# A fused two-block kernel on one core: key norms inverted with tokens on partitions, two gate projections inside the first RWKV tile, the rest of the RG-LRU spread over tiles 1 to 6

## The chip, the cores and the metric

The kernel is written for one core of a Trainium2 chip, and nothing else runs. The metric is the device time of one execution in microseconds (us), lower is better. The engines are named as in the profile: PE is TensorE (matrix products), PEld its weight loads, DVE is VectorE, ACT is ScalarE, POOL is GpSimd, SP is SyncE, which issues most of the transfers. Each works through its own list of instructions in order; semaphores tie them together.

## The reference, cut to what matters

Two model blocks run one after the other on 1024 tokens of width 1024, in float32. The change lies in the first. It projects the tokens, mixes them in three ways side by side (windowed attention, RG-LRU, RWKV-7), gates each with the silu of a projection, projects out and normalises. The two ways that the change touches:

```python
# RG-LRU (256 channels)
xc = causal_conv(xb, width 4) + conv_b
r, i = sigmoid(xc @ wa + ba), sigmoid(xc @ wx + bx)      # blocks of 64
log_a = -8 * r * softplus(-lam);  a = exp(log_a)
u = sqrt(-expm1(2 * log_a)) * (i * xc)
h[t] = a[t] * h[t-1] + u[t]                               # scan over tokens
# RWKV-7 (4 heads of 64)
kk = k * k_k
kk = kk * rsqrt(sum(kk ** 2 over a head) + 1e-12)
k = k * (1 + (a - 1) * k_a)
state = state * w + (state @ -kk) b^T + v k^T;  y = state @ r     # b = kk * a
bonus = sum(r * k * r_k over a head) * v
out = concat(y_a * silu(g_a), h * silu(g_b), (norm(y) + bonus) * silu(g_c)) @ w_out
```

The second block (pooling mixer, latent attention, two layers of routed experts) takes the rest of the time and is not touched.

## The kernel before

Data of the first block lie with channels on partitions and the 1024 tokens along the free axis, as two tiles (`j` = 0, 1) of 128 channels each. Three stages matter, and every engine has a function for each.

**Attention with projections beside it** (`pe_swa` and others) ends near 338 us. `proj` lists all projections, each a group of eight float32 products of 128x512 accumulated in one of two PSUM banks (ring `pj`). The last six, `left[0]` to `left[5]`, are gates. `act_project` takes the sigmoid of one, and `dve_project` multiplies it (line 379), which frees the bank.

**Preparation** (`pe_prep`, `act_prep`, `dve_prep`) works on whole 128x1024 tensors. PE does, in this order: `left[0]`; sums of squares of `kk` over a head (four products with `pair_ones`, ring `pr_`, six banks); eight products for the decay and `a` (`DECAY`); `left[1]`, four products of the RG-LRU's two gates for `j` = 0 (`LRU_MM`), `left[2]`, four for `j` = 1, `left[3]`, `left[4]`, two for the bonus (`rk`), `left[5]`, two more. DVE does the convolution (`dve_conv`, lines 777 and 780), the reciprocal of the norms (798), the running sum of the log decay (803) and the products with decays (820 to 825), a 128x1024 instruction each. ACT takes roots (747), sigmoids (752, 761), exponentials (764 to 768), and the RG-LRU's tanh and exp (771, 772). `after_prep` is what all three wait for before the next stage.

**RWKV tiles** (`pe_rwkv`, `act_rwkv`, `dve_rwkv`): eight tiles of 128 tokens. `rounds()` gives the order: tile `i` does steps 0 to 9 (its front: products of 64x64 that invert a triangular matrix) in rounds 10i to 10i+9, and in the same rounds tile `i`-1 does steps 10 to 19 (its back: the state recurrence and the norm). So tile 0's rounds hold a front alone. Between two rounds' products PE waits for a copy on ACT (1205) or a combination on DVE (1271). Step 0 begins with four masks on DVE (1259, 1265), behind the previous tile's step 19, a reciprocal (1356) that waits for a root on ACT (1240). `dve_lru` and `act_lru` put what is left of the RG-LRU between these, all with `i` = 0: products 848, 852, 854 and 859 in steps 0 to 8, the scans (863) in steps 9 and 11, the last products (867) in steps 13 and 16. Steps 10 and above fall in tile 1's rounds. When the RG-LRU is done (`lru_v`), SP loads the output weights, eight transfers of 512 KB (`sp_rwkv`). Tile 7 waits for them from step 10 on and does part of the output projection between its steps.

Of the kernel before, what the change touches and what calls it, by code (L numbers as in the profile page):

```python
# [170 lines left out]
def build(nc, io):  # L171
    ctx = ExitStack()
    with ctx:
# [164 lines left out]
        def pe_project(e, n):  # L338
            group, c0, width, half, kind, _ = proj[n]
            if n == first_of[group]:  # L340
                e.wait_ge(*m_w[group])
# [296 lines left out]
        def sp_first(e):  # L638
# [13 lines left out]
            for name, before in (("rk", None), ("vwa", "ga"), ("lru", "rk"), ("gc", "vwa")):  # L652
                if before:
# [37 lines left out]
        order = [(("kk", j, hf), "S") for j in range(2) for hf in range(2)] + [(("wa",) + x, "S") for x in DECAY]  # L691
        order += [(("lru",) + x, "S") for x in LRU_MM] + [(("rk", j, hf), "V") for j in range(2) for hf in range(2)]
        pr_ = Banks(banks[:6], *sw.rest(), order)
        reset_in, masks_in, lru_zero = signal("reset"), signal("rwkv_masks"), signal("lru_zero")
# [4 lines left out]
        assert len(left) == 6

        def pe_prep(e):
            pe_project(e, left[0])
            wait_all(e, after_swa)
            for j in range(2):
# [23 lines left out]
            for j in range(2):  # L728
                e.wait_ge(*rk_in.at(j + 1))
                for hf in range(2):  # L730
                    key = ("rk", j, hf)
                    wait_all(e, pr_.free(key))
                    mm(e, pr_.bank[key], pair_ones, tmp[j][:, half_cols(hf)], True, True).then_inc(*pr_.fill(key))
                if j == 0:
                    pe_project(e, left[5])

        def act_prep(e):
            wait_all(e, after_swa)
            for j in range(2):
                e.wait_ge(*kk_raw.at(j + 1))  # L740
                e.activation(Lc[:, j, :], kk[:, j, :], ACT.Square).then_inc(*kk_sq.up())
            act_project(e, left[0])
            for j in range(2):
                for hf in range(2):
                    key = ("kk", j, hf)
                    e.wait_ge(*pr_.full(key))
                    e.activation(tmp[j][:, half_cols(hf)], pr_.bank[key], ACT.Sqrt, bias=eps_kk).then_inc(*pr_.drain(key, "S"))
            for j, what, hf in DECAY:
# [3 lines left out]
                e.activation(dst[:, j, half_cols(hf)], pr_.bank[key], ACT.Sigmoid, bias=col(bias, j)).then_inc(*pr_.drain(key, "S"))  # L752
            for j in range(2):
# [2276 lines left out]
```

## Time and profile before

| | |
|---|---|
| runs | 2324.21, 2327.46, 2329.42 us; median 2327.46 |
| profiled execution | 2327.86 us, its span 2326.1 us |
| PE busy | 2114.3 us, 91% of the span |
| DVE, ACT, POOL busy | 826.3, 559.5, 198.5 us |
| preparation | from about 346 to 415 us |
| RWKV tiles | from 415 to about 605 us |

The span is the time from the first to the last instruction in the profiled execution. A float32 product shows as two PE records. The granted clock is a share of TensorE's full speed: 1.00 is 2.4 GHz, 0.50 is 1.2 GHz.

### The profile page before, as it was taken

The page shows a single profiled execution, that of the slowest core. Times are in us where ns is not written, and L with a number is a line of the kernel's source. Part 1 is how long each engine was busy: PE and PEld are TensorE (multiplying, and loading weights), DVE is VectorE, ACT ScalarE, POOL GpSimd, SP SyncE. Part 2 cuts the span into 40 slices and gives each one's busy share as a digit, 9 for nine tenths or more (in the row PEclk, how much of TensorE's full clock was granted, in tenths as well). Part 3 has the DMA queues.
Part 4 walks back from the last instruction along what each step waited for, and adds up shares of the span by engine and source line. Part 5 has one row for each costly group of instructions (what it writes and reads, how often), then busy time and mean ns, then how long its engine had stood idle before and what let it go on. Part 6 is the DMA issues. An engine that isn't in the chain of part 4 may idle for free. (4 is left out here: it accounts for less than half of the span.)

```text
span 2326.1 us, 27337 instructions
## 1 busy us (share of the span) xinstructions
PE 2114.3 (91%) x10876; PEld 1217.8 (52%) x10876; DVE 826.3 (36%) x1833; ACT 559.5 (24%) x1349; POOL 198.5 (9%) x297
## 2 busy tenths in 40 slices
PE   8999999789989669999987999999999849999991
PEld 4545554687438344444434657767764324444440
DVE  1115549664344332111125533443431141111115
ACT  1013235332113201112213433333321101111112
POOL 0000002011432010000002000000000000000003
PEclk9999999899989779999998999999999869999996
DMA  3501000100211359999963000000100067999966
GB/s 127 217 23 37 19 2 3 74 4 3 70 60 44 124 218 369 384 408 367 365 241 125 21 0 1 1 1 1 73 13 36 36 253 299 367 367 366 370 271 245
DMA packets 46199, 349.30 MB, mean 150 GB/s; under 512 B 6256, under 2 KB 6576, under 8 KB 36208
## 3 DMA queue, kind: packets, MB, share of 16 engines
q1 hardware_dynamic: 32176, 296.97, 32.5%
q0 software_dynamic: 13888, 50.47, 6.2%
q8 instruction: 92, 1.51, 0.3%
q14 instruction: 43, 0.35, 0.0%
HBM read 292.82 MB, written 54.59 MB: 149 GB/s over the span
## 5 line engine op out<-in xcount | busy, mean ns | idle before, releaser
L202 PE MATMUL psum<-arena 128*128 128x512 f32 (+7 forms) x9328 | 1956.8, 384 | 113.9 <-DVE arena L1923 25.9
L202 PEld LDWEIGHTS psum<-arena 128*128 128x128 f32 (+3 forms) x9328 | 1046.0, 169 | 955.1 <-issue 831.5
L2054 DVE TENSOR_TENSOR arena<-psum,arena 128x256 f32<-128x256 f32 x64 | 27.2, 425 | 539.9 <-ACT arena L2098 539.9
L2134 POOL DMA_INDIRECT arena<-xn_rows,arena x64 | 60.2, 941 | 818.7 <-PE psum L2021 587.4
L2098 ACT ACTIVATE arena<-psum 128x256 f32<-128x256 f32 x64 | 24.6, 384 | 400.9 <-PE psum L202 400.9
L1475 ACT ACTIVATE arena<-arena 128x1024 f32<-128x1024 f32 x43 | 45.4, 1056 | 250.9 <-DVE arena L2789 101.6
L2702 ACT ACTIVATE arena<-psum,arena 128x1024 f32<-128x1024 f32 (+8 forms) x72 | 50.2, 699 | 188.6 <-DVE arena L2738 188.6
L2091 ACT ACTIVATE arena<-psum 128x512 f32<-128x512 f32 x64 | 38.2, 597 | 185.5 <-PE psum L202 185.5
L2021 PE MATMUL psum<-arena 128*128 128x128 f32 x512 | 68.2, 277 | 9.8 <-DMA arena<-xn_rows,arena 9.8
L1205 ACT ACTIVATE arena<-psum 128x256 f32<-128x256 f32 (+3 forms) x128 | 45.6, 369 | 106.8 <-PE psum L202 96.7
L2121 DVE COPY arena<-psum 128x512 f32<-128x512 f32 x64 | 44.3, 692 | 61.5 <-PE psum L202 61.5
L2021 PEld LDWEIGHTS psum<-arena 128*128 128x128 f32 x512 | 59.3, 144 | 11.2 <-DMA arena<-xn_rows,arena 10.1
L2079 ACT ACTIVATE arena<-psum 128x512 f32<-128x512 f32 x64 | 38.2, 598 | 93.2 <-PE psum L2021 93.2
L2731 DVE TENSOR_TENSOR psum<-psum,arena 128x128 f32<-128x128 f32 (+2 forms) x72 | 20.3, 282 | 103.5 <-PE psum L202 103.2
L2733 DVE TENSOR_REDUCE arena<-psum 128x1 f32<-128x1024 f32 (+8 forms) x72 | 50.8, 706 | 2.5
L2242 DVE SCALAR_TENSOR_TENSOR arena<-arena 128x1024 f32<-128x1024 f32 (+1 forms) x34 | 43.5, 1280 | 21.4 <-DMA arena<-expert_rows,arena 19.7
L2754 DVE COPY arena<-psum 128x512 f32<-128x512 f32 (+3 forms) x48 | 22.8, 490 | 76.0 <-PE psum L2657 75.9
L2248 POOL DMA_INDIRECT arena<-expert_rows,arena x34 | 34.4, 1012 | 178.9 <-issue 126.3
L2657 PE MATMUL psum<-arena 128*128 128x128 f32 x352 | 48.9, 273 | 0.0
L2114 DVE COPY arena<-psum 128x512 f32<-128x512 f32 x64 | 43.5, 680 | 11.6 <-PE psum L2021 11.6
L365 ACT ACTIVATE arena<-psum 128x512 f32<-128x512 f32 (+1 forms) x26 | 15.5, 597 | 128.5 <-PE psum L202 128.5
L379 DVE TENSOR_TENSOR arena<-psum,arena 128x512 f32<-128x512 f32 x16 | 10.9, 689 | 87.5 <-ACT arena L360 87.4
(286 smaller groups left out, 1288.9 us busy)
## 6 DMA issues: line engine op xcount, KB each, us to landing
arena<-in_w_exp SPq DMA_DIRECT2D x64, 3072.0 KB, 11.7
expert_rows<-arena SPq DMA_DIRECT2D x80, 512.0 KB, 4.1
arena<-in_x SPq DMA_DIRECT2D x16, 512.0 KB, 4.2
xn_rows<-arena SPq DMA_DIRECT2D x16, 512.0 KB, 2.6
arena<-in_w_out SPq DMA_DIRECT2D x8, 512.0 KB, 7.9
arena<-in_w_o SPq DMA_DIRECT2D x1, 4096.0 KB, 12.0
out<-arena SPq DMA_DIRECT2D x8, 512.0 KB, 5.8
arena<-in_rows SPq DMA_DIRECT2D x6, 512.0 KB, 6.3
```

The lines of the kernel that those rows point to most:

```text
L202: return e.matmul(out, lhsT, rhs, start=start, stop=stop, skip_group_check=True)
L1205: e.activation(dst, src, ACT.Copy, bias=0.0).then_inc(*ring.drain((i, name), "S"))
L1475: return e.activation(junk, h[:, s, :], ACT.Square, accum_out=sq_sum[:, s:s + 1])
L2021: m = e.transpose(four(ring.bank[key])[:, k, :], xe[:, P * (4 * hf + k):P * (4 * hf + k + 1)], ident)
L2079: e.activation(y.xt[b % 2][:, 4:8, :], four(y.ex.bank[key]), ACT.Copy, bias=0.0).then_inc(*y.ex.drain(key, "S"))
L2114: e.tensor_copy(y.xt[b % 2][:, 0:4, :], four(y.ex.bank[key])).then_inc(*y.ex.drain(key, "V"))
L2121: e.tensor_copy(y.y[b % 3][:, half_cols(0)], y.ex.bank[key]).then_inc(*y.ex.drain(key, "V"))
L2134: e.indirect_dma_start(out=xe, out_offset=None, in_=xn_dram[:, :], in_offset=bass.IndirectOffsetOnAxis(idx.bitcast(I32)[:, block:block + 1 ...
L2242: e.scalar_tensor_tensor(out=h[0:n, s, :], in0=c[j][0:n, :], scalar=gates[0:n, s, j:j + 1], in1=h[0:n, s, :], op0=ALU.mult, op1=ALU.add).t ...
L2657: m = e.transpose(four(sd.bank[key])[:, j, :], pb[:, kp:kp + P], ident)
L2702: e.activation(pb[0:n, p0:p1], part_bank(key).bank[key][0:n, 0:p1 - p0], ACT.Exp, bias=mx[0:n, 0:1], scale=SCALE, accum_out=rsu[0:n, u:u + ...
L2733: e.tensor_reduce(mx[0:n, u:u + 1], bk[0:n, 0:p1 - p0], AX.X, ALU.max).then_inc(*V.up())
```

## The change

Norms of the keys: the squares (ACT now takes them from `k` itself, with `k_k` as its scale) become the stationary operand of sixteen narrow products against two columns of `pair_ones`, so 32 sums per token lie in one bank with tokens on partitions (`kn`). Root and reciprocal then run on 128x32. ACT widens the result to 128x1024 twice (`kk_b`, in the memory of `Em`), and sixteen products with the identity turn it back into four PSUM banks (`kk`), which DVE multiplies into `kk`. The first tap of the convolution moves from DVE to ACT. ACT's exponentials now stand ahead of the RG-LRU's sigmoids, and tanh and exp leave the stage. The bonus products stand before `left[2]`. `left[4]` and `left[5]` move into tile 0: two products at the head of each of steps 1 to 8, sigmoid and multiplication at step 9. The rest of the RG-LRU moves to tiles 1 to 6 by two tables. The names of memory areas change with it, and the waits of tile 1 for `lru_u` go.

```diff
+def pe_project(e, n, part=range(KD)):
-    wait_all(e, pj.free(n))
+    if part[0] == 0:
+        wait_all(e, pj.free(n))
-    for k in range(KD):
+    for k in part:
         i = mm(e, out, w_view[group][:, k, c0:c0 + width], xT[:, k, half_cols(half)], k == 0, k == KD - 1)
+    if part[-1] == KD - 1:
+        i.then_inc(*pj.fill(n))
...
+order = [("kn", "S")] + [(("wa",) + x, "S") for x in DECAY] + [(("kk", j, hf), "V") for j in range(2) for hf in range(2)]
+for j in range(2):
+    order += [(("lru",) + x, "S") for x in LRU_MM if x[1] == j]
+    if j == 0:
+        order += [(("rk", jj, hf), "V") for jj in range(2) for hf in range(2)]
...
+LATE = left[4:]
+LATE_AT = {step: (LATE[(step - 1) // 4], range(2 * ((step - 1) % 4), 2 * ((step - 1) % 4) + 2)) for step in range(1, 9)}
...
-        e.wait_ge(*kk_sq.at(j + 1))
-        for hf in range(2):
-            key = ("kk", j, hf)
-            wait_all(e, pr_.free(key))
-            mm(e, pr_.bank[key], pair_ones, Lc[:, j, half_cols(hf)], True, True).then_inc(*pr_.fill(key))
+    e.wait_ge(*kk_sq.at(2))
+    wait_all(e, pr_.free("kn"))
+    for t in range(NT):
+        for j in range(2):
+            m = mm(e, pr_.bank["kn"][:, 4 * t + 2 * j:4 * t + 2 * j + 2], Lc[:, j, P * t:P * (t + 1)], pair_ones[:, 0:P:HD], True, True)
+    m.then_inc(*pr_.fill("kn"))
...
+    pe_project(e, left[1])
+    e.wait_ge(*kk_wide.at(2))
     for j in range(2):
-        pe_project(e, left[1 + j])
+        for hf in range(2):
+            key = ("kk", j, hf)
+            wait_all(e, pr_.free(key))
+            for u in range(4):
+                c = 4 * (4 * hf + u) + 2 * j
+                m = mm(e, four(pr_.bank[key])[:, u, :], kk_b[:, c:c + 2, :].rearrange("p a b -> p (a b)"), ident, True, True)
+            m.then_inc(*pr_.fill(key))
...
+    for j in range(2):
+        if j:
+            pe_project(e, left[2])
...
+        if j == 0:
+            for jj in range(2):
+                e.wait_ge(*rk_in.at(jj + 1))
+                for hf in range(2):
+                    key = ("rk", jj, hf)
+                    wait_all(e, pr_.free(key))
+                    mm(e, pr_.bank[key], pair_ones, tmp[jj][:, half_cols(hf)], True, True).then_inc(*pr_.fill(key))
     pe_project(e, left[3])
-    pe_project(e, left[4])
...
-        e.activation(Lc[:, j, :], kk[:, j, :], ACT.Square).then_inc(*kk_sq.up())
+        e.activation(Lc[:, j, :], R[2 + j], ACT.Square, scale=col("k_k", j)).then_inc(*kk_sq.up())
+    e.wait_ge(*pj.full(last_of["vwa"]))
+    for j in range(2):
+        e.wait_ge(*pj.empty(last_half["xb", j]))
+        e.activation(xc[:, j, :], xb[:, j, 0:T], ACT.Identity, bias=col("conv_b", j), scale=col("conv_w", 4 * j)).then_inc(*conv_in.up())
...
+    e.wait_ge(*pr_.full("kn"))
+    e.activation(kk_dev, pr_.bank["kn"][:, 0:4 * NT], ACT.Sqrt, bias=eps_kk).then_inc(*pr_.drain("kn", "S"))
...
+    e.wait_ge(*kk_in.at(1))
+    for c in (0, 2 * NT):
+        e.activation(kk_b[:, c:c + 2 * NT, :], bc_last(kk_r[:, c:c + 2 * NT], HD), ACT.Copy, bias=0.0).then_inc(*kk_wide.up())
+    for j in range(2):
+        e.wait_ge(*scanned.at(j + 1))
+        e.activation(Ep[:, j, :], Lc[:, j, :], ACT.Exp, scale=-EXP_HALF).then_inc(*exped.up())
+        e.wait_ge(*pr_.full(("kk", 1, 1)))
+        e.activation(Em[:, j, :], Lc[:, j, :], ACT.Exp, scale=EXP_HALF).then_inc(*exped.up())
+    for j in range(2):
+        e.wait_ge(*to_exp.at(j + 1))
+        e.activation(sgm[:, j, :], sgm[:, j, :], ACT.Exp, scale=-EXP_HALF).then_inc(*exped.up())
...
-        e.wait_ge(*pr_.empty(("lru", "x", 1, 1)))
-        e.activation(q_[:, j, :], ra[:, j, :], ACT.Tanh, scale=ncl[:, j:j + 1]).then_inc(*S.up())
-        e.activation(ra[:, j, :], ra[:, j, :], ACT.Exp, scale=cl[:, j:j + 1]).then_inc(*lru_a.up())
-    for n in left[3:]:
-        act_project(e, n)
+    act_project(e, left[3])
...
-    e.tensor_scalar(xc[:, j, :], xb[:, j, 0:T], col("conv_w", 4 * j), col("conv_b", j), ALU.mult, ALU.add).then_inc(*V.up())
+    e.wait_ge(*conv_in.at(j + 1))
...
-        dve_conv(e, j)
-        if j == 0:
-            dve_project(e, left[0])
+        e.tensor_scalar(kk[:, j, :], R[2 + j], col("k_k", j), None, ALU.mult).then_inc(*V.up())
...
+    e.wait_ge(*pr_.empty("kn"))
+    e.reciprocal(kk_r, kk_dev).then_inc(*kk_in.up())
...
-        e.reciprocal(tmp[j], tmp[j]).then_inc(*V.up())
-        e.wait_ge(*V.last())
-        e.tensor_tensor(kk[:, j, :], kk[:, j, :], tmp[j], ALU.mult).then_inc(*V.up())
...
-        e.tensor_tensor(av[:, j, :], av[:, j, :], kk[:, j, :], ALU.mult).then_inc(*V.up())
...
+    for j in range(2):
+        for hf in range(2):
+            key = ("kk", j, hf)
+            kc = kk[:, j, half_cols(hf)]
+            e.wait_ge(*pr_.full(key))
+            e.tensor_tensor(kc, pr_.bank[key], kc, ALU.mult).then_inc(*pr_.drain(key, "V"))
...
+    for j in range(2):
+        e.tensor_tensor(av[:, j, :], av[:, j, :], kk[:, j, :], ALU.mult).then_inc(*V.up())
+    dve_bonus(e, 0)
...
+LRU_ACT = {(1, 2): ("tanh", 0), (1, 4): ("decay", 0), (1, 6): ("tanh", 1), (1, 8): ("decay", 1), (3, 6): ("sqrt", 0), (4, 2): ("sqrt", 1)}
+LRU_DVE = {(1, 4): ("gate", 0), (1, 9): ("gate", 1), (2, 4): ("square", 0), (2, 9): ("rest", 0), (3, 4): ("square", 1), (3, 9): ("rest", 1),
+           (4, 4): ("input", 0), (4, 9): ("scan", 0), (5, 2): ("input", 1), (5, 4): ("scan", 1), (5, 9): ("out", 0), (6, 2): ("out", 1)}
...
+after_prep = pr_.totals + [pj.empty(left[3]), (prep_v.sem, 2), (exped.sem, 6), (rk_in.sem, 2), m_lru]
...
+        if i == 0 and s in LATE_AT:
+            pe_project(e, *LATE_AT[s])
+        if (i, s) == (0, 10):
+            wait_all(e, pj.totals)
...
+        act_lru(e, i, s)
+        if (i, s) == (0, 9):
+            for n in LATE:
+                act_project(e, n)
...
+        dve_lru(e, i, s)
+        if (i, s) == (0, 9):
+            for n in LATE:
+                dve_project(e, n)
+            e.memset(STt[:, 0], 0.0).then_inc(*states.up())
```

In the diff, `dve_bonus(e, j)` holds the two multiplications of line 832, unchanged. `gate`, `square`, `rest`, `input`, `scan` and `out` are the operations of lines 848, 852, 854, 859, 863 and 867.

How the instructions stand on PE from the end of attention to tile 1. Before (80 products of 128x512 are the preparation; L1078 are tile transposes):

```order
L202 MATMUL psum<-arena 128x512 x80
L202 MATMUL psum<-arena 64x64 x16
L1078 MATMUL psum<-arena 128x128 x8
L202 MATMUL psum<-arena 64x64 x152
L1078 MATMUL psum<-arena 128x128 x8
L202 MATMUL psum<-arena 64x64 x184
```

In the changed kernel:

```order
L202 MATMUL psum<-arena 128x512 x16
L202 MATMUL psum<-arena 128x2 x16
L202 MATMUL psum<-arena 128x512 x16
L202 MATMUL psum<-arena 128x128 x16
L202 MATMUL psum<-arena 128x512 x28
L202 MATMUL psum<-arena 64x64 x16
L1120 MATMUL psum<-arena 128x128 x8
L202 MATMUL psum<-arena 128x512 x2
L202 MATMUL psum<-arena 64x64 x16
L202 MATMUL psum<-arena 128x512 x2
L202 MATMUL psum<-arena 64x64 x24
```

The preparation has 20 wide products fewer and 32 small ones more, and 16 of the wide ones stand in pairs within tile 0 (the first two pairs are shown).

DVE in tile 0, after the masks of step 0. Before:

```order
L848 TENSOR_TENSOR arena<-arena 128x1024
L1289 TENSOR_TENSOR arena<-arena 128x256
L1276 COPY arena<-psum 128x256
L848 TENSOR_TENSOR arena<-arena 128x1024
L1265 TENSOR_TENSOR arena<-psum,arena 128x3x128 x2
L852 TENSOR_TENSOR arena<-arena 128x1024
L854 SCALAR_TENSOR_TENSOR arena<-arena 128x1024
L1276 COPY arena<-psum 128x256
```

In the changed kernel the 128x1024 instructions are gone there (same operations, other line numbers):

```order
L1328 TENSOR_TENSOR arena<-arena 128x256
L1317 COPY arena<-psum 128x256
L1306 TENSOR_TENSOR arena<-psum,arena 128x3x128 x2
L1317 COPY arena<-psum 128x256
L1312 TENSOR_TENSOR arena<-arena,psum 128x256 x3
```

DVE in tile 2 of the changed kernel, rounds 4 to 9, where two of them now stand (889 and 892; before, there was none in tile 2):

```order
L1312 TENSOR_TENSOR arena<-arena,psum 128x256
L889 TENSOR_TENSOR arena<-arena 128x1024
L1358 SCALAR_TENSOR_TENSOR arena<-psum,arena 64x128 x2
L1312 TENSOR_TENSOR arena<-arena,psum 128x256
L1369 SCALAR_TENSOR_TENSOR arena<-psum,arena 128x64 x2
L1377 TENSOR_SCALAR arena<-arena 128x64 x2
L1384 TENSOR_TENSOR arena<-psum,arena 128x2x64 x2
L1389 SCALAR_TENSOR_TENSOR arena<-psum,arena 128x2x128
L1312 TENSOR_TENSOR arena<-arena,psum 128x512
L892 SCALAR_TENSOR_TENSOR arena<-arena 128x1024
L1395 RECIPROCAL arena<-arena 128x256
```

One stands between a front combination and the recurrence's copy, the other ahead of the norm's reciprocal.

## Rows read from the trace of the kernel before

**Rows 1.** Timeline of PE: start us, us, instruction, idle before and its releaser

```profile
402.26 11.93 PE L202 MATMUL psum<-arena 128*128 128x512 f32 x20 [3.68 <-DVE arena L379]
415.12 0.69 PE L202 MATMUL psum<-arena 64*64 64x64 f32 x32 [0.93 <-DVE arena L832]
...
424.04 1.61 PE L202 MATMUL psum<-arena 64*64 64x64 f32 x48 [2.55 <-issue]
```

**Rows 2.** Windows: PE, PEld, DVE, ACT, POOL busy, granted clock, DMA share, GB/s

```profile
360.50:363.00 2.50, 2.50 (x4) 1.08 (x4) 2.50 (x1) 2.14 (x4) 1.89 (x9) 0.54 0.03 7
402.00:404.00 2.00, 1.74 (x2) 0.84 (x3) 2.00 (x4) 0.00 (x0) 0.00 (x0) 0.50 0.00 0
465.00:469.00 4.00, 1.93 (x39) 1.93 (x40) 0.93 (x3) 0.08 (x1) 0.00 (x0) 0.69 0.02 6
```

**Rows 3.** Windows from the first mask of one tile to the next, tiles 0 to 6

```profile
415.90:437.30 21.40, 13.95 (x319) 12.56 (x319) 16.66 (x22) 7.26 (x13) 0.00 (x0) 0.81 0.01 2
437.30:456.80 19.50, 17.41 (x483) 15.79 (x481) 15.70 (x35) 7.30 (x20) 0.00 (x0) 0.95 0.18 55
456.80:477.90 21.10, 16.76 (x468) 15.46 (x464) 11.65 (x33) 6.45 (x19) 2.31 (x4) 0.92 0.39 154
477.90:495.30 17.40, 15.57 (x470) 14.33 (x468) 11.62 (x32) 6.53 (x19) 2.31 (x4) 1.00 0.02 4
495.30:512.90 17.60, 15.57 (x472) 14.50 (x468) 11.58 (x32) 6.59 (x19) 2.31 (x4) 1.00 0.02 4
512.90:530.00 17.10, 15.59 (x472) 14.50 (x468) 11.51 (x32) 6.58 (x19) 2.30 (x4) 1.00 0.01 4
530.00:547.10 17.10, 15.67 (x472) 14.57 (x468) 11.51 (x32) 6.58 (x19) 2.31 (x4) 1.00 0.01 3
```

**Rows 4.** Groups by form on PE, 100 to 110 us: busy us, mean ns, idle

```profile
L202 PE MATMUL psum<-arena 128*128 128x512 f32 x15 | 6.6, 592 | 0.0
L202 PE MATMUL psum<-arena 128*128 128x128 f32 x37 | 4.3, 275 | 0.0
```

**Rows 5.** Timeline of ACT in the preparation

```profile
369.43 0.60 ACT L360 ACTIVATE arena<-psum 128x512 f32<-128x512 f32 x1 [6.79 <-PE psum L202]
370.29 0.69 ACT L761 ACTIVATE arena<-psum,arena 128x512 f32<-128x512 f32 x1 [0.26 <-PE psum L202]
...
383.87 1.28 ACT L764 ACT_TABLE_LOAD   x1
...
387.07 1.04 ACT L764 ACTIVATE arena<-arena 128x1024 f32<-128x1024 f32 x1
388.02 1.04 ACT L765 ACTIVATE arena<-arena 128x1024 f32<-128x1024 f32 x1
```

**Rows 6.** Timeline of DVE in the preparation

```profile
358.19 6.55 DVE L798 RECIPROCAL arena<-arena 128x1024 f32<-128x1024 f32 x1
...
392.43 1.23 DVE L820 TENSOR_TENSOR arena<-arena 128x1024 f32<-128x1024 f32 x1
```

**Rows 7.** Timeline of DVE in tile 3: rounds 34 and 35, then round 39

```profile
485.96 0.42 DVE L1271 TENSOR_TENSOR arena<-arena,psum 128x256 f32<-128x256 f32 x1
486.41 0.50 DVE L1319 SCALAR_TENSOR_TENSOR arena<-psum,arena 64x128 f32<-64x128 f32 x2
487.40 0.42 DVE L1271 TENSOR_TENSOR arena<-arena,psum 128x256 f32<-128x256 f32 x1 [0.49 <-PE psum L202]
...
493.18 1.75 DVE L1356 RECIPROCAL arena<-arena 128x256 f32<-128x256 f32 x1 [0.35 <-ACT arena L1240]
```

**Rows 8.** Timelines of DVE and PE: a scan in tile 1, the wait at tile 3's start

```profile
440.49 2.28 DVE L863 TENSOR_TENSOR_SCAN arena<-arena 128x1024 f32<-128x1024 f32 x1
...
479.38 2.90 PE L202 MATMUL psum<-arena 64*64 64x64 f32 x123 [1.15 <-DVE arena L1265]
```

**Rows 9.** Timeline of PE in tile 2, and the issues of the output weights

```profile
467.07 3.13 PE L202 MATMUL psum<-arena 64*64 64x64 f32 x58 [2.33 <-issue]
...
arena<-in_w_out SPq DMA_DIRECT2D x8, 512.0 KB, 7.9
```

More of the change, by code:

```diff
@@ L666, in build @@
         reset = take(T)
-        end_prep = top[0]
+        kk_dev, kk_r = take(4 * NT), take(4 * NT)
+        kk_b = Em.rearrange("p a b -> p (a b)").rearrange("p (a b) -> p a b", b=HD)
+        assert top[0] <= base_sums
         yb = Lc
@@ L816, in dve_prep @@
                                        op1=ALU.mult).then_inc(*rk_in.up())
+            for j in range(2):
[4 more added lines that the diff above has]
+                    e.tensor_tensor(kc, pr_.bank[key], kc, ALU.mult).then_inc(*pr_.drain(key, "V"))
+            dve_project(e, left[1])
+            e.wait_ge(*pr_.empty(("kk", 1, 1)))
+            for j in range(2):
+                e.tensor_tensor(av[:, j, :], av[:, j, :], kk[:, j, :], ALU.mult).then_inc(*V.up())
+            dve_bonus(e, 0)
             e.wait_ge(*rk_in.last())
+            e.wait_ge(*V.last())
             for j in range(2):
@@ L825, in dve_prep @@
                 e.tensor_tensor(kk[:, j, :], kk[:, j, :], sgm[:, j, :], ALU.mult).then_inc(*prep_v.up())
-            for n in left[3:5]:
-                dve_project(e, n)
-            for j in range(2):
-                for hf in range(2):
-                    key = ("rk", j, hf)
-                    e.wait_ge(*pr_.full(key))
-                    e.tensor_tensor(bonus[:, j, half_cols(hf)], pr_.bank[key], R[4 + j][:, half_cols(hf)],
-                                    ALU.mult).then_inc(*pr_.drain(key, "V"))
-                if j == 0:
-                    dve_project(e, left[5])
@@ L837, in act_lru, with dve_bonus @@
-        def act_lru(e, step):
-            if step in (5, 6):
-                j = step - 5
+            dve_bonus(e, 1)
+            dve_project(e, left[2])
+            dve_project(e, left[3])
+        def dve_bonus(e, j):
+            for hf in range(2):
+                key = ("rk", j, hf)
+                e.wait_ge(*pr_.full(key))
+                e.tensor_tensor(bonus[:, j, half_cols(hf)], pr_.bank[key], R[4 + j][:, half_cols(hf)], ALU.mult).then_inc(*pr_.drain(key, "V"))
+        LRU_ACT = {(1, 2): ("tanh", 0), (1, 4): ("decay", 0), (1, 6): ("tanh", 1), (1, 8): ("decay", 1), (3, 6): ("sqrt", 0), (4, 2): ("sqrt", 1)}
@@ new lines, in build, with act_lru @@
+        LRU_DVE = {(1, 4): ("gate", 0), (1, 9): ("gate", 1), (2, 4): ("square", 0), (2, 9): ("rest", 0), (3, 4): ("square", 1), (3, 9): ("rest", 1),
+                   (4, 4): ("input", 0), (4, 9): ("scan", 0), (5, 2): ("input", 1), (5, 4): ("scan", 1), (5, 9): ("out", 0), (6, 2): ("out", 1)}
+        def act_lru(e, i, s):
+            what, j = LRU_ACT.get((i, s), (None, None))
+            if what == "tanh":
+                e.wait_ge(*pr_.empty(("lru", "x", 1, 1)))
+                e.activation(q_[:, j, :], ra[:, j, :], ACT.Tanh, scale=ncl[:, j:j + 1]).then_inc(*S.up())
+            elif what == "decay":
+                e.activation(ra[:, j, :], ra[:, j, :], ACT.Exp, scale=cl[:, j:j + 1]).then_inc(*lru_a.up())
+            elif what == "sqrt":
@@ L841, in act_lru, with dve_lru @@
                 e.wait_ge(*lru_q.at(j + 1))
                 e.activation(q_[:, j, :], q_[:, j, :], ACT.Sqrt).then_inc(*lru_sq.up())
-        def dve_lru(e, step):
-            if step in (0, 1):
-                j = step
+        def dve_lru(e, i, s):
+            what, j = LRU_DVE.get((i, s), (None, None))
+            if what == "gate":
                 e.wait_ge(*pr_.empty(("lru", "x", 1, 1)))
                 e.tensor_tensor(ib[:, j, :], ib[:, j, :], xc[:, j, :], ALU.mult).then_inc(*V.up())
-            elif step in (2, 3):
-                j = step - 2
+            elif what == "square":
@@ L855, in dve_lru @@
                                        op1=ALU.mult).then_inc(*lru_q.up())
-            elif step in (7, 8):
-                j = step - 7
+            elif what == "input":
                 e.wait_ge(*lru_sq.at(j + 1))
-                e.tensor_tensor(ib[:, j, :], ib[:, j, :], q_[:, j, :], ALU.mult).then_inc(*lru_u.up())
-            elif step in (9, 11):
-                j = (step - 9) // 2
-                e.wait_ge(*lru_u.last())
+                e.tensor_tensor(ib[:, j, :], ib[:, j, :], q_[:, j, :], ALU.mult).then_inc(*V.up())
+            elif what == "scan":
+                e.wait_ge(*V.last())
                 e.tensor_tensor_scan(xc[:, j, :], ra[:, j, :], ib[:, j, :], 0.0, ALU.mult, ALU.add).then_inc(*V.up())
-            elif step in (13, 16):
-                j = (step - 13) // 3
+            elif what == "out":
                 e.wait_ge(*V.last())
@@ L1280, in dve_rwkv @@
                         e.wait_ge(*bk_.full((i - 2, "var")))
-                    if i == 1:
-                        e.wait_ge(*lru_u.last())
                     for par in range(2):
```

75 lines of the change are left out of this document (20 added, 55 removed).

## The prediction

> **What bounds the kernel now.** The first view is the whole page: PE is busy for nine tenths of the span, so a change pays only where it takes work, waiting or half-speed time from PE. The change moves work inside one stretch, 346 to 605 us, so the second view is the timeline of PE there. It shows the preparation as nearly unbroken work up to 398.6 us. Then PE waits 3.68 us for DVE, works off ten products in 11.93 us, waits 0.93 us and starts tile 0 at 415.12 [rows 1]. Ten wide products should take ten times two records of 6.6/15 = 0.44 us, that is 8.8 us [rows 4]; the granted clock is 0.50 behind the wait [rows 2], so about 3.1 us are lost to the half clock (1.2 GHz).
>
> The third view is the table of windows by tile [rows 3]. Tiles 3 to 6, which hold no RG-LRU, take 17.1 to 17.6 us, 17.3 in the mean, of which PE is busy 15.6. Tile 0, with a front alone, takes 21.4 with PE busy 13.95 at a mean clock of 0.81. Its waits are for DVE, which works through the RG-LRU's 128x1024 products there: 2.55 us before the product at 424.04 [rows 1]. Tile 1, with both scans, takes 19.5. Tile 2 takes 21.1 without any of the RG-LRU; there PE stands 2.33 us on "issue" while the output weights land, and the clock falls behind it to 0.69 [rows 2, 9]. I take that excess of about 3.7 us as a late instruction fetch behind the burst.
>
> **The preparation.** Work on PE: sixteen wide products of `left[4]` and `left[5]` leave, and four of the norms. A product is 0.88 us, so -14.1 and -3.5. Added are sixteen 128x128 products with the identity at two records of 4.3/37 = 0.116 us, +3.7 [rows 4]. The sixteen narrow ones have two columns, which no row shows. They cannot cost more than the 128-column ones, 3.7 us; from below the 64x64 products run at 3.13 us for 58 records, 0.054 each, or 1.7 us for 32 [rows 9]. Each still has a full weight load, so I take 3.0, near the upper end. The Trainium skill, "TensorE: Matmul & The Clock Gate", section "LDWEIGHTS (loading the stationary operand)", counts the columns of the stationary operand over 1.2 in ns, 107 ns for 128; by it 32 loads would be 3.4 us and the total 0.4 us more. Sum of the work: -14.1 - 3.5 + 3.7 + 3.0 = -10.9.
>
> Waits of PE: before, 3.68 + 0.93 = 4.6. After, DVE no longer sets them: two reciprocals of 6.55 us [rows 6] shrink to one of 128x32, and the 128x1024 products of 1.23 us stay at about their number. But ACT now stands in the way. The exponential into `Em` overwrites `kk_b`, so it must wait for the last identity product. `left[1]`'s sigmoid began at 369.43 [rows 5]; that product ends half a microsecond sooner, the identity products 3.7 later, at 372.6. Then ACT runs five instructions at the 0.95 spacing of the exponentials, a table load of 1.28, the sigmoid of `left[1]` at 0.60 and the first of the RG-LRU at 0.69 [rows 5]: 372.6 + 4.8 + 1.3 + 0.6 + 0.7 = 380.0. The third bonus product needs the bank that this last one frees. PE gets there after four and two wide products, 372.6 + 5.3 = 377.9, and waits 2.1 us, with the hop some 2.3. The last wait, for sigmoid and multiplication of `left[3]`, was 0.93 behind a shorter chain and becomes about 1.7. So 4.0 us of waits, -0.6.
>
> Clock: before 3.1 us lost behind a wait of 3.68. After a wait of 2.33 tile 2 lost 3.7 - 2.3 = 1.4. For 2.3 us I take 1.6, so -1.5. In both kernels there is a dip at 360.5 behind the 32-row products [rows 2]; I leave it equal. Preparation: -10.9 - 0.6 - 1.5 = **-13.0**; from -10.5 (full loss of clock) to -16 (none, narrow products cheap).
>
> **Tile 0.** Its work at full clock is 13.95 x 0.81 = 11.3 us [rows 3]. The late products add 14.1, and stand where PE waited for ACT and DVE, each pair longer (1.8 us) than a combination's return trip of 1.2 (the wait and the 0.42 copies in [rows 7, 8]). Only step 9 has none, 1.1 us of waiting. 11.3 + 14.1 + 1.1 = 26.5 against 21.4: **+5.1**. The clock stays at 1.00, since PE is dense.
>
> **The RG-LRU in tiles 1 to 6.** Ten products of 1.23 us and two scans of 2.28 [rows 6, 8] go between a steady tile's instructions. An inserted one costs its length less the idle time that DVE has at that place. At step 9 DVE has 0.35 us idle before the reciprocal [rows 7], and what follows, the masks, is what PE waits 1.15 us for already [rows 8]. So a product costs 0.8 (spacing 1.15 less 0.35) and a scan 1.85. At step 4 there is no idle ahead of the recurrence's copy at 486.41, and 0.49 after it [rows 7]: 0.65 for a product, 1.7 for the scan. At step 2 I take 0.35, by the same reading. Tile 1 also gets a table load for the root at step 18, behind an exponential: 0.7 more at its end, and 0.7 at its start, where DVE works off `left[4]` and `left[5]` ahead of the masks. ACT's other instructions fall into its idle time. Against [rows 3], from a base of 17.3:
>
> tile 1: 17.3 + 0.7 + 0.65 + 1.5 = 20.15, +0.65
> tile 2: 17.3 + 0.65 + 0.8 = 18.75, -2.35 (the weights' burst leaves it)
> tile 3: the same 18.75, +1.35
> tile 4: 17.3 + 0.65 + 1.85 = 19.8, +2.2
> tile 5: 17.3 + 0.35 + 1.7 + 0.8 = 20.15, +3.05
> tile 6: 17.3 + 0.35 + 3.7 (the burst comes here) = 21.35, +4.25
>
> Together **+9.15**. The RG-LRU's share is 10.75 us of 16.9 us of instructions. From below: tile 1 before holds a scan and two products, 4.7 us, and exceeds 17.3 by 2.2, of which 1.0 is the clock (0.95 of 19.5), so a quarter shows, 4.3 us in all; from above, all but the idle ones, 14. I keep 10.75, since steps 4 and 9 are tighter places than those. The weights are asked for in round 62, and needed in round 80, 31 us later by the tiles' pace, so they cost no wait. What follows 605 us is chained to the last tile, and shifts.
>
> **Sum.** -13.0 + 5.1 + 9.15 = +1.25 us. On the profiled execution's 2327.86 us that is 2329.1; the median of the runs is 0.4 us lower, so I forecast 2328.7: no change that shows. A measurement of this kernel can tell about 0.2%, 4.7 us, from none.
>
> **Rivals.**
> *The clock falls at the long seams.* At the ends of tiles 1 and 4 PE would wait 1.15 + 1.5 = 2.65 and 1.15 + 1.85 = 3.0 us for the masks. Waits of 3.68 and 2.33 us were followed by half speed [rows 1, 2, 9]. Each such fall costs 1.4 to 3.1. With 3.1 at both the time is 2334.9, slower by over 0.2%; it decides once the two falls together pass 3.5 us. For it: the rows. Against: the 1.15 us waits in tiles 3 to 6 leave the clock at 1.00, and these tiles are otherwise dense. 0.34, which also holds costlier insertions.
> *The RG-LRU hides well.* If all twelve cost as little as tile 1 shows, 4.3 us, the time is 2328.7 - 6.45 = 2322.3, faster by 0.2%. For it: tile 1, whose last product at step 16 sits before an idle DVE. Against: the chain at steps 4 and 9. With a preparation at the short end (-16) it is 2319. 0.25 in all.
> *No burst in tile 6.* If the fetch is not late there, 3.7 us go: 2325.0, no change that shows. 0.1, within the forecast's chance.
> *The late projections aren't hidden.* If tile 0 kept its waits, it would be 21.4 + 14.1 less the regained clock of 2.6, 32.9 us, 6.4 more, 2335.1. Against it speaks that each step's waits are on ACT and DVE alone. 0.04, in the slower share.
>
> **Chances and range.** Forecast, within 0.2%: 0.41, its own range 2323 to 2332. Slower 0.34, faster 0.25. Low end 2319 (the hidden RG-LRU and the short preparation), high end 2337 (both falls, and insertions dearer by 2).
>
> **What would show it.** Right: PE's first tile product 13 us earlier than 415.12, at about 402; a wait of 2 us in the bonus products, on ACT; tile 0 at 26 to 27 us with the clock at 1.00; tiles 3 to 5 between 18.5 and 20.5; a wait of 1.9 to 2.0 us for the masks at the ends of tiles 2 and 3; an "issue" gap with the weights' burst in tile 6 and none in tile 2. Wrong: clock below 1.00 in tiles 4 and 5, or tiles 2 to 5 at 17.5.

## The result, and the profile after

The change makes the kernel slower: 2343.15 us (median of 4 runs, 2339.6 to 2345.18) against 2327.76 us of the kernel before in the same session, ratio 1.0067, 95% interval 1.0055 to 1.0079. The forecast was 2328.7, with 2319 to 2337 as its range. The profiled execution is the slowest of the four, 2345.18 us; its span is 2343.5.

I measure the changed stretch from one DVE instruction that both kernels have at the preparation's entry to the first reciprocal behind tile 7 (608.24 us before, 621.44 after). First the entry, in the timeline of DVE before, then after:

```profile
346.64 0.16 DVE L786 TENSOR_SCALAR arena<-arena 128x2 f32<-128x2 f32 x1
```

```profile
346.88 0.16 DVE L812 TENSOR_SCALAR arena<-arena 128x2 f32<-128x2 f32 x1
```

So the stretch is 261.60 us long before and 274.56 after, +12.96. It adds up from four pieces, each from trace marks: preparation to the first mask -10.04, tile 0 +6.46, tiles 1 to 6 +16.28, tile 7 and its close +0.26.

Timeline of PE after, in the preparation and at the tiles' seams (start, us, instruction, wait ahead and its releaser), to be read beside [rows 1, 8, 9]:

```profile
345.44 35.04 PE L202 MATMUL psum<-arena 128*128 128x512 f32 x124
382.84 20.82 PE L202 MATMUL psum<-arena 128*128 128x512 f32 x44 [2.36 <-ACT arena L798]
405.33 0.69 PE L202 MATMUL psum<-arena 64*64 64x64 f32 x32 [1.67 <-issue]
...
455.86 8.66 PE L202 MATMUL psum<-arena 64*64 64x64 f32 x264 [2.08 <-DVE arena L1306]
...
476.00 7.43 PE L202 MATMUL psum<-arena 64*64 64x64 f32 x264 [1.84 <-DVE arena L1306]
...
494.93 8.76 PE L202 MATMUL psum<-arena 64*64 64x64 f32 x264 [1.85 <-DVE arena L1306]
...
516.77 5.64 PE L202 MATMUL psum<-arena 64*64 64x64 f32 x168 [2.89 <-DVE arena L1306]
...
528.89 6.79 PE L202 MATMUL psum<-arena 64*64 64x64 f32 x128 [2.10 <-DVE arena L1358]
...
552.05 4.33 PE L202 MATMUL psum<-arena 64*64 64x64 f32 x100 [1.57 <-issue]
...
559.35 0.58 PE L202 MATMUL psum<-arena 64*64 64x64 f32 x24 [1.92 <-issue]
```

The waits stand where they were forecast, and all but one in the size forecast: the one at tile 2's start is 2.08 us (2.65 forecast). The wait of 2.10 us in the middle of tile 5 was in the sum as 1.7 us of the scan, and was not named as a wait. What is new is in the last columns of the windows (granted clock, DMA share, GB/s):

```profile
354.00:358.00 4.00, 4.00 (x24) 2.88 (x25) 3.93 (x4) 2.29 (x4) 0.00 (x0) 0.77 0.01 4
358.00:366.00 8.00, 8.00 (x16) 3.35 (x13) 4.86 (x4) 5.99 (x10) 2.87 (x5) 0.50 0.02 4
384.00:386.00 2.00, 2.00 (x4) 0.93 (x3) 2.00 (x3) 0.43 (x1) 0.00 (x0) 0.50 0.00 0
456.00:458.00 2.00, 2.00 (x48) 2.00 (x50) 0.74 (x3) 0.39 (x1) 1.03 (x2) 0.50 0.03 8
518.00:520.00 2.00, 2.00 (x57) 2.00 (x58) 0.42 (x1) 0.75 (x3) 0.00 (x0) 0.50 0.00 0
530.00:534.00 4.00, 4.00 (x70) 3.75 (x67) 1.25 (x6) 1.31 (x4) 0.00 (x0) 0.57 0.00 0
```

The clock is at its lower level of 1.2 GHz behind the narrow products (from 356 to 366 us, with PE busy throughout), behind the wait of 2.36 us, and in tiles 2, 4 and 5. Windows by tile, answering to [rows 3], tiles 0 to 6:

```profile
406.13:433.97 27.84, 26.15 (x352) 15.35 (x351) 7.02 (x16) 5.64 (x13) 0.00 (x0) 1.00 0.01 2
433.97:454.35 20.38, 16.82 (x480) 15.15 (x480) 13.86 (x34) 13.23 (x25) 0.00 (x0) 1.00 0.01 4
454.35:474.49 20.14, 16.90 (x464) 15.71 (x464) 13.79 (x35) 6.58 (x18) 2.31 (x4) 0.92 0.01 3
474.49:493.42 18.93, 15.68 (x464) 14.49 (x464) 13.70 (x35) 7.53 (x19) 2.31 (x4) 1.00 0.01 3
493.42:515.25 21.83, 17.16 (x464) 16.00 (x464) 14.89 (x34) 7.53 (x19) 2.30 (x4) 0.92 0.01 3
515.25:539.06 23.81, 18.46 (x464) 17.35 (x464) 15.87 (x36) 6.58 (x18) 2.31 (x4) 0.86 0.01 3
539.06:560.04 20.98, 14.49 (x442) 13.41 (x443) 12.70 (x33) 5.50 (x16) 3.11 (x6) 1.00 0.54 203
```

### The profile page after: what moved, and what is told of

Same layout as the page of the kernel before. It is cut to its first block and busy times, and to the rows that moved or that the text cites. A ratio compares the mean times of both kernels' runs of the same rounds, so it can differ in the third digit from the quotient of the medians.

```text
span 2343.5 us, 27446 instructions
## 1 busy us (share of the span) xinstructions
PE 2126.0 (91%) x10932; PEld 1229.1 (52%) x10932; DVE 812.7 (35%) x1832; ACT 562.3 (24%) x1351; POOL 203.1 (9%) x297
## 5 line engine op out<-in xcount | busy, mean ns | idle before, releaser
L202 PE MATMUL psum<-arena 64*64 64x64 f32 (+9 forms) x9384 | 1969.6, 386 | 116.9 <-DVE arena L1966 25.9
L202 PEld LDWEIGHTS psum<-arena 128*128 128x128 f32 (+3 forms) x9384 | 1058.2, 172 | 958.6 <-issue 845.9
## 6 DMA issues: line engine op xcount, KB each, us to landing
arena<-in_w_exp SPq DMA_DIRECT2D x64, 3072.0 KB, 12.3
```

Source lines behind the costliest of these rows:

```text
L202: return e.matmul(out, lhsT, rhs, start=start, stop=stop, skip_group_check=True)
```

## The experiments

Twelve kernels in three sessions; the kernel before took 2329.52, 2330.09 and 2327.6 us in them (29 runs each). "Stretch" is the length defined above; it and the lengths of tiles come from one profiled execution of each kernel, the times and ratios from all its runs.

### 65 columns in place of 2

```diff
-m = mm(e, pr_.bank["kn"][:, o:o + 2], Lc[...], pair_ones[:, 0:P:HD], True, True)      # o = 4 * t + 2 * j
+m = mm(e, pr_.bank["kn"][:, o:o + 65], Lc[...], pair_ones[:, HD - 1:P], True, True)
```

> The changed kernel, but the sixteen narrow products run against 65 columns instead of 2 (the first two are the same, the other 63 land in columns that are overwritten or not read; the two-column ones took 0.11 us a record, the 128-column ones 0.116, so the time on the engine is the same). Theory N (the two-column products let TensorE fall to its half clock): the half-clock stretch from 356 to 366 us shrinks towards that of before, 360.5 to 364, tile 0 starts 2.5 to 3.5 us earlier, time 3 us below the changed kernel. Rival (the 32-row products behind them do it, as before the change): same stretch, no change within 0.5 us at tile 0's start.

2334.18 us, ratio 1.002 [1.0008, 1.0033]; stretch 268.80, 5.8 shorter than the change's. It starts tile 0 6.0 us sooner after its entry, where I expected 2.5 to 3.5. The groups by form in the preparation (busy us, mean ns), after, and then here:

```profile
L202 PE MATMUL psum<-arena 32*128 32x512 f32 x16 | 7.1, 1050 | 0.0
...
L202 PE MATMUL psum<-arena 128*128 128x2 f32 x32 | 3.6, 249 | 0.0
```

```profile
L202 PE MATMUL psum<-arena 32*128 32x512 f32 x16 | 4.4, 606 | 0.0
...
L202 PE MATMUL psum<-arena 128*128 128x65 f32 x32 | 3.7, 273 | 0.0
```

The narrow products cost 3.7 us in place of 3.6. The 32-row products behind them take 4.4 us in place of 7.1, and the window of eight us reads 1.00:

```profile
358.00:366.00 8.00, 8.00 (x25) 3.62 (x22) 7.10 (x6) 7.97 (x12) 4.32 (x7) 1.00 0.05 12
...
379.49 19.12 PE L202 MATMUL psum<-arena 128*128 128x512 f32 x44 [1.70 <-ACT arena L798]
```

The wait of 2.36 is 1.70 here, and the 44 records behind it take 19.12 and not 20.82: no half clock there either. From entry to the first tile product it is 52.42 us (58.45 in the change, 68.48 before), so without the falls the preparation gives 16.1 us. The width of the narrow products decides whether the clock falls here. That they would do it alone is not shown: the kernel before has none, and had a shorter dip of its own at the same 32-row products [rows 2].

Not all of it reaches the end of the stretch. Tiles 1 to 6 are 1.6 us longer here (127.63 against 126.07), above all tile 3, which had no fall in the changed kernel and has one here, behind the same wait of 1.84 us:

```profile
469.12:489.57 20.45, 17.20 (x464) 16.00 (x464) 13.69 (x35) 7.54 (x19) 2.32 (x4) 0.92 0.01 3
```

### The RG-LRU's DVE work at steps 6 and 7

```diff
-LRU_DVE = {(1, 4): ("gate", 0), (1, 9): ("gate", 1), (2, 4): ("square", 0), (2, 9): ("rest", 0), ...
-           (4, 4): ("input", 0), (4, 9): ("scan", 0), (5, 2): ("input", 1), (5, 4): ("scan", 1), (5, 9): ("out", 0), (6, 2): ("out", 1)}
+LRU_DVE = {(1, 6): ("gate", 0), (1, 7): ("gate", 1), (2, 6): ("square", 0), (2, 7): ("rest", 0), ...
+           (4, 6): ("input", 0), (4, 7): ("scan", 0), (5, 6): ("input", 1), (5, 7): ("scan", 1), (6, 2): ("out", 0), (6, 6): ("out", 1)}
```

> The changed kernel with the RG-LRU's DVE products and scans at steps 6 and 7 of tiles 1 to 5 (the two last at steps 2 and 6 of tile 6) instead of steps 4 and 9. Theory S (a step costs its length less DVE's idle time at its place, 0.7 to 0.8 at steps 6 and 7, and beyond that what the half clock takes behind long waits of PE for the masks): tiles 1 to 5 shorter by 0.3 to 0.5 us for a product, the clock at 1.00 in tiles 2 and 4, sum 5 to 8 us below the changed kernel. Rival (the RG-LRU's work costs what DVE is busy, wherever it stands): within 2 us of the changed kernel.

2329.66 us, ratio 1.0005 [0.9995, 1.0015]; stretch 262.65, 11.9 shorter. Tiles 4 and 5, which hold the scans:

```profile
489.55:508.24 18.69, 15.85 (x470) 14.54 (x466) 14.56 (x35) 7.65 (x20) 2.30 (x4) 1.00 0.01 3
508.24:527.28 19.04, 15.62 (x466) 14.50 (x464) 14.71 (x34) 6.59 (x19) 2.31 (x4) 1.00 0.01 3
```

Tile 4 holds the same two instructions as in the changed kernel and is 3.1 us shorter than with steps 4 and 9. Tile 5 is 4.8 us shorter, and has one product less, which now stands in tile 6. In both the clock stays at 1.00. Over all it is more than the 5 to 8 us that I expected.

### The same instructions on two columns

```diff
-e.tensor_tensor(ib[:, j, :], ib[:, j, :], xc[:, j, :], ALU.mult)
+e.tensor_tensor(ib[:, j, 0:2], ib[:, j, 0:2], xc[:, j, 0:2], ALU.mult)      # and so the other five kinds
```

> The changed kernel with every RG-LRU instruction of DVE in tiles 1 to 6 cut to two columns of each half (the RG-LRU's result is left out but for these; the instructions, waits and ACT's work stay). It prices all of the spread work on DVE. My prediction had 10.75 us for it without the clock; with the clock falls seen behind the long waits theory S expects 15 to 18 us less than the changed kernel, tiles 2 to 5 at 17.3 to 17.6 us and the clock at 1.00 there. Rival (the tiles are long for another reason, the new memory places or ACT's instructions): under 8 us less.

2325.44 us, ratio 0.9981 [0.9971, 0.9992]; stretch 258.44. Against it, steps 6 and 7 cost 262.65 - 258.44 = 4.2 us and steps 4 and 9 cost 274.56 - 258.44 = 16.1 us. The two kernels' medians are 4.2 us apart as well. In tiles 1 to 6 alone the difference of steps 6 and 7 is only 2.0 us (113.19 against 111.23), but that leaves out a part: here the output weights land in tile 6 (20.24 us), with steps 6 and 7 they land in part in tile 7, which with its close is 2.3 us longer. In tiles 1 to 5 alone it is 3.2 us for the ten instructions there, and 14.1 for the eleven with steps 4 and 9.

My expectation held for the sum and missed in the tiles: tiles 2, 4 and 5 take 18.51, 17.98 and 18.27 us, not 17.3 to 17.6. In tile 2 the clock reads 0.91, and PE's wait for the masks at its start is 2.08 us, as in the changed kernel. So the RG-LRU's product on DVE does not make this wait. Ahead of it ACT runs the last of the RG-LRU's exponentials (1.13 us) and loads the table for the root (1.28 us). DVE's reciprocal waits for that root, behind a product of two columns that has long ended:

```profile
448.68 0.15 DVE L886 TENSOR_TENSOR arena<-arena 128x2 f32<-128x2 f32 x1
450.62 1.75 DVE L1395 RECIPROCAL arena<-arena 128x256 f32<-128x256 f32 x1 [1.79 <-ACT arena L1280]
```

With steps 6 and 7 the wait of 2.08 and the clock of 0.91 in tile 2 stand too.

### The late projections back in the preparation

```diff
-LATE = left[4:]
+LATE = []
-    pe_project(e, left[3])
+    for n in left[3:]:
+        pe_project(e, n)
...
```

ACT's and DVE's parts of the two projections move with them.

> The changed kernel with the last two gate projections back at the end of the preparation. Theory: tile 0 starts 14 to 16 us later (sixteen wide products of 0.88 and one wait for a bank), and lasts 18 to 20 us instead of 27.8, so the kernel is 5 to 7 us slower than the changed one: the move itself gains. Rival (the late products only swap places): within 2 us.

2342.08 us, ratio 1.0054 [1.0035, 1.0073]. My expectation missed. Counted from its own entry the first mask comes 12.3 us later, and tile 0 shrinks by 12.97, from 27.84 to 14.87 (with a fall, clock 0.86): the two nearly change places. The stretch is 2.0 us longer, with more falls in the tiles behind.

### Both mends together

The edits of the first two experiments.

> The changed kernel with both mends: narrow products against 65 columns, and the RG-LRU at steps 6 and 7. The first alone started tile 0 5.0 us earlier (401.1 against 406.1), the second alone shortened tiles 1 to 6 from 126.1 to 113.2 us. If they add, tile 0 starts at 401, tiles 1 to 6 take 113 us, and the kernel is 17 to 18 us below the changed one, 3 to 5 us below the kernel before. Rival (they overlap, since both act through TensorE's clock): 13 to 15 us below the changed one, level with before.

2326.07 us, ratio 0.9984 [0.9973, 0.9995]; stretch 255.88. This version is faster than the kernel before by 0.16%, and than the changed one by 0.8% (by their two ratios). The two mends add: 5.8 + 11.9 = 17.7 expected, 18.7 seen.

### The norms part alone

The norms, the order of ACT's exponentials and the bonus products as in the change; projections and RG-LRU as before.

> The changed kernel with the two other parts undone: both late projections at the end of the preparation, the RG-LRU's products in tiles 0 and 1 as before, tanh and exp in the preparation. What is left is the norms with tokens on partitions, the convolution's first tap on ACT and the new order in the preparation. The kernel with the late projections undone started tile 0 at 419.0, 3.1 later than the kernel before; tile 0 and 1 should then take what they took before, 21.4 and 19.5. Theory (the norms' part does not shorten PE's path: 7.3 us of products for 3.5, and the half clock behind the two-column ones): 3 to 7 us slower than before. Rival (it frees DVE of 13 us and so helps): faster than before by 3 or more.

2333.68 us, ratio 1.0019 [1.001, 1.0028]; stretch 263.72, 2.1 longer than before. With two columns, the norms part costs time by itself, and behind the narrow products the clock is low here too (0.57 from 354 to 366 us).

### The spread RG-LRU alone

The kernel before, with the RG-LRU's rest in tiles 1 to 6, at steps 6 and 7.

> The kernel before with one part of the change alone, the RG-LRU's rest in tiles 1 to 6, at steps 6 and 7. Tile 0 then has no 128x1024 product of DVE and should take 14.9 us as with the late projections undone (21.4 before); tiles 1 to 6 take 113.2 against 109.8 before. Sum -6.5 + 3.4: 3 us below the kernel before, and 0 to 2 more from the tanh and exp that leave ACT in the preparation. Rival (tile 0's gain is eaten in the later tiles and by the weights' burst): within 1 us of before.

2330.1 us, ratio 0.9997 [0.9987, 1.0007]; stretch 263.21. Tile 0 falls from 21.38 to 13.70 us, and the gain is eaten behind it: tiles 1 to 6 take 114.20 us (109.79 before), and tile 7 with its close takes 66.15 (61.14 before). There PE stands on "issue" while the last of the output weights land:

```profile
544.94 3.22 PE L202 MATMUL psum<-arena 64*64 64x64 f32 x133 [1.15 <-DVE arena L1263]
551.75 10.48 PE L202 MATMUL psum<-arena 64*64 64x64 f32 x223 [3.59 <-issue]
```

### Filler products at the seams, twice

```diff
+    if i:
+        wait_all(e, fr.free((i, "p2a")))
+        for _ in range(4):
+            mm(e, fr.bank[i, "p2a"][:, 256:512], ident, kk[:, 0, 0:256], True, True)
```

> The changed kernel, RG-LRU at steps 4 and 9 as it is, with four added products of 128x256 (0.44 us each, results unused) on PE in the wait for the masks at the start of tiles 1 to 7. Theory K (the waits of 1.85 to 2.9 us at the tile seams let the clock fall, which costs 1.4 to 3 us each in tiles 2, 4 and 5): the clock there rises to 0.97 or more but for the fall inside tile 5 behind the recurrence's wait, tiles 2 and 4 get shorter by 0.5 to 1.5 us though PE has more to do. Rival (the clock falls for another reason, or the tiles are long by DVE's work alone): tiles 1 to 7 as long or longer by up to 0.5 us each, the clock unchanged.

2342.48 us, ratio 1.0053 [1.004, 1.0066], and inconclusive: the fillers' bank comes free only by the first mask, so they ran behind much of the wait. The clock reads 1.00 in tiles 2 to 4, but the fillers took time of their own: tile 4 is 0.6 us shorter, tile 2 is not, and tile 3, which had no fall, is 1.9 longer. The second try uses the free half of another bank, right behind the last product ahead of the masks:

```diff
+    if 1 <= i <= 5:
+        wait_all(e, bk_.free((i, "gt_0")))
+        for _ in range(4):
+            mm(e, bk_.bank[i, "gt_0"][:, 256:512], ident, kk[:, 0, 0:256], True, True)
```

> The changed kernel, with the RG-LRU's work still at steps 4 and 9, and with four extra 128x256 products that nothing reads (0.44 us of PE each when they run back to back), issued right behind the x64 product of tiles 1 to 5, into the bank of gt_0 that is free there. So they lie inside the wait for the masks at the seam (2.08, 1.84, 1.85, 2.89 and 1.85 us in the changed kernel), not behind it. If the fall of the clock to 0.50 behind the seam is a cost of its own beside the wait, the clock is 1.00 in tiles 2 and 4 (0.92 before) and in the seam of tile 5, and tiles 2 and 4 come out 1 to 1.5 us shorter than 20.14 and 21.83. If VectorE alone sets these tiles (the masks come late whatever PE does), their lengths stay within 0.4 us while the clock reads 1.00.

2336.69 us, ratio 1.004 [1.0026, 1.0054]. The timeline shows the wait filled (2.08 us at this place after the change), and the windows show tiles 2 to 5:

```profile
450.66 2.61 PE L202 MATMUL psum<-arena 64*64 64x64 f32 x24
453.43 7.50 PE L202 MATMUL psum<-arena 64*64 64x64 f32 x264 [0.16 <-DVE arena L1310]
...
451.92:470.90 18.98, 17.40 (x473) 15.71 (x472) 13.91 (x34) 6.59 (x18) 2.31 (x4) 1.00 0.01 3
470.90:489.87 18.97, 17.58 (x474) 15.93 (x473) 13.70 (x35) 7.54 (x19) 2.31 (x4) 1.00 0.01 3
489.87:509.88 20.01, 18.62 (x479) 16.83 (x478) 14.74 (x35) 7.54 (x19) 2.31 (x4) 1.00 0.01 4
509.88:532.34 22.46, 18.00 (x469) 16.40 (x468) 15.87 (x36) 6.59 (x18) 2.31 (x4) 0.92 0.01 2
```

The masks of tile 2 come no sooner (tile 1 takes 20.36 us, 20.38 in the changed kernel), yet tiles 2, 4 and 5 are 1.16, 1.82 and 1.35 us shorter, while tile 3, which had no fall, is the same. This is the clock's price, apart from the wait's. The stretch is 7.15 us shorter; 1.6 of it lies in the preparation, where in this execution no fall followed a wait of 2.35 us (19.12 us for the 44 records).

### The output weights spread out

```diff
+    e.wait_ge(*fr.full([(6, "xt"), (6, "q32"), (6, "pb"), (6, "q64"), (7, "p2a"), (7, "p4a"), (7, "p8"), (7, "akv")][k]))      # ahead of transfer k
```

> The kernel with both mends (norms against 65 columns, the RG-LRU's work at steps 6 and 7), with the eight transfers of the output weights no longer issued in one burst: each waits on SyncE for one product of tiles 6 and 7, spread over both. If the burst delays PE's instructions, the stretches of issue of 0.73 and 1.02 us on PE in tiles 6 and 7 go, and the time falls by 1 to 2 us from 2326.07. If they have another cause (PE's own order at the last seam), they stay and the time is within 0.5 us of it. If the weights now land too late for the output projection, a wait for them shows behind tile 7 and the time is longer.

2323.94 us, ratio 0.9986 [0.9977, 0.9995], against 0.9984 with both mends. One stretch of issue (0.73 us) is gone and the other is 0.58 in place of 1.02. Tile 7 with its close is 1.4 us shorter (60.93 against 62.30) and the stretch 1.6 (254.25 against 255.88). So the burst has a part in these small gaps. That is the gain expected, in one execution of each; the ratios don't show it, and can't tell 1 to 2 us.

### Both mends, projections in the preparation

> The kernel with both mends, with the two last gate projections back in the preparation: it prices the move of the projections with a clock of 1.00 on both sides. If the two only change places (as 12.9 us of preparation stood against 12.97 us of tile 0 with the change's own preparation), the time is within 2 us of 2326.07. If the move gives what the forecast gave it (14.1 us of preparation against 5.1 us more in tile 0), it is 7 to 9 us longer.

2325.14 us, ratio 0.9988 [0.9976, 1.0]; stretch 256.15 against 255.88. Here tile 0 holds a front and nothing else, at full clock:

```profile
412.89:426.49 13.60, 10.28 (x313) 9.24 (x313) 5.79 (x14) 3.78 (x9) 0.00 (x0) 1.00 0.01 2
```

With the projections it takes 27.84: 14.24 us more, for 14.1 us of products, and the preparation is 13.8 us shorter. Moving them is worth nothing.

### The norms part alone, 65 columns

> The kernel before with the norms part of the change alone, and the 32 norm products against 65 columns in place of 2. If the clock's fall behind the narrow products is all that their width costs, tile 0 starts near 410.8 us in place of 415.8 (norms part alone, 2 columns), and the time is 4 to 5 us under its 2333.68 us, 1 us or so under the kernel before. If 65 columns only move the fall to tile 0, the start comes earlier and the time stays.

2327.91 us, ratio 0.9995 [0.9985, 1.0005]. The stretch is 260.10, 3.6 shorter than with two columns and 1.5 shorter than before. Each start has to be read from its own entry: 66.15 us to the first tile product, against 70.49 with two columns. The clock reads 1.00 in both 350 to 366 and 366 to 404 us. Tile 0 takes back a part: 22.41 us at a clock of 0.66 (21.38 at 0.80 before), and 22.39 at 0.66 with two columns.

## Why the prediction was wrong

**The step that failed** is the clock, at two places: "In both kernels there is a dip at 360.5 behind the 32-row products; I leave it equal", and the +9.15 for tiles 1 to 6, which counted DVE's instructions but no fall of the clock.

*Preparation, -13.0 forecast, -10.04 measured.* The waits were as forecast (2.3 and 1.7; 2.36 and 1.67 seen), and the narrow products' own cost was nearly so (3.0; 3.6 seen). The Trainium skill's "TensorE: Matmul & The Clock Gate", section "LDWEIGHTS (loading the stationary operand)", which would have had 3.4 us for the 32 loads, was the nearer; the trace agrees with it. Also as forecast, 20.82 - 19.12 = 1.7 us went to half speed behind the wait in the bonus products (1.6). But the dip was not equal. Before, PE lost 2.5 x 0.46 = 1.2 us in [rows 2]'s window and 0.6 in the two us behind it (clock 0.72). After, it lost 4 x 0.23 + 8 x 0.5 = 4.9 us. The difference of 3.1 is about the whole error of the preparation, 3.0. I took the 32-row products for the cause of the dip; the run with 65 columns leaves them as they are and has no dip at all. Why the kernel before has one stays open.

*Tile 0, +5.1 forecast, +6.46 measured.* The sum took the front at 11.3 us of work with most of its waits covered. A front alone takes 13.6, and the projections come on top at full price (14.24). On balance they covered no wait. What tile 0 gains, 7.7 us, it gains from the RG-LRU's leaving, as the run with that part alone shows. That the projections' move brings nothing was not among the rivals; "the late projections aren't hidden" named the mechanism, but put its price at 6.4 us more than the forecast, where it is 1.3.

*Tiles 1 to 6, +9.15 forecast, +16.28 measured.* The instructions were priced nearly right. The forecast's 10.75 is 10.05 for the twelve and 0.7 for ACT's table load; in tiles 1 to 5, which hold eleven of them, it is 9.7. Measured there, the run with fillers is 9.8 us longer than the one with two columns. This is rough, since each has a fall of its own left, in tile 5 and in tile 2. The fillers gave back 4.8 us in tiles 1 to 6 (126.07 to 121.26). By tiles the forecast was 20.15, 18.75, 18.75, 19.8, 20.15 and 21.35; with fillers the tiles took 20.36, 18.98, 18.97, 20.01, 22.46 and 20.48. Only tile 5 is off by more than 1 us, and it still has a wait of 2.1 us in its middle behind the scan at step 4, with a fall behind it. So the seams were as long as forecast or shorter, the clock fell behind some of them, and that is what the sum left out. At tile 2's start the sum added a product on DVE and a table load on ACT; they stand side by side, and ACT alone sets the wait. The burst in tile 6 came as forecast (20.98 against 21.35).

*The rivals.* "The clock falls at the long seams" is what happened. It named two seams, at the starts of tiles 2 and 5; the falls came there, at tile 4's start behind a wait of only 1.85 us, and in the middle of tile 5. With its 3.1 us for each of two it would have come to 2334.9. Three falls that the fillers took away gave back 1.2 to 1.8 us each. "The RG-LRU hides well" is false for steps 4 and 9 (16.1 us) and true for steps 6 and 7 (4.2 us shown for twelve instructions). The bound that I drew from tile 1 before (4.3 us) was right for such places, and would have been a reason to ask where else they could stand.

*What stays open.* The stretch explains 13.0 of the 15.4 us between the medians. The two profiled executions are 17.3 us apart; of these 13.0 lie in the stretch and 4.2 behind it, where the kernels are the same. What follows the stretch takes 1717.9 us before, 1722.1 after, and between these two in every other trace. I have no cause for the 2.4 us that remain, and did not look for one by a run. Nor is it shown why the same wait is followed by a fall in one trace and not in another, or why the projections in tile 0 cover none of its waits.

## What to carry to other kernels

Price a wait on PE and the fall of the clock behind it as two terms, and give the second a chance at every wait as long as those that were followed by one here, from 1.57 us up, even if another as long passed without. Ask of each inserted DVE instruction whether the next product waits for what stands behind it: two rounds earlier or later, the same twelve instructions cost 4.2 us in place of 16.1. Ask the same of ACT: a table load ahead of the root made a wait that no placing on DVE could take away. And where a move puts work "beside" a stage, measure first how much of that stage is waiting; a stage of 13.6 us in which PE is busy for 10.3 has 3.3 us of waits to offer to 14 us of work, and here not even these were won.

## What the runs showed of the hardware

Behind products with two moving columns the clock fell although PE reads as busy: 16 products of 128x2 (32 records, 3.6 us) were followed by about 10 us at 1.2 GHz, and against 65 columns, for 3.7 us, the clock stayed at 2.4. Two pairs of kernels that differ in this alone show it, with the whole change and with the norms part alone. In both the 32-row products stand behind the narrow ones; narrow products without them were not run. "TensorE: Matmul & The Clock Gate" of the Trainium skill says, in "What's actually happening", that the gate follows how busy PE has been. The busy share in this profile (8.00 of 8.00 us at 0.50) does not show it, so that share can't be used to rule a fall out.

The fall behind a wait is no fixed matter of its length: waits of 1.84 and 1.85 us stand at the starts of tiles 3 and 4, and in the changed kernel's trace only the second is followed by a fall. With 65 columns the first is too, though nothing in tiles 1 to 3 was changed: tile 3 took 20.45 us at 0.92, and 18.93 at 1.00 without the fall. 2.36 us was followed by a fall in the changed kernel's trace, 2.35 in that with fillers was not. The shortest wait seen with a fall behind it is one of 1.57 us on "issue", in tile 6 of the run with two columns on DVE (clock 0.50 from 538 to 540 us); one of 1.57 us in tile 6 of the changed kernel had none.
